# Gates of two token blocks by indirect transfers, those of the third by matmul

## The reference, cut to what matters

```python
def peer_ffn(xn, w_query, sub_keys, u, v):
    q = (xt @ w_query).reshape(T, H, 2, PEER_HALF)
    s = jnp.einsum('thpd,hpkd->thpk', q, sub_keys)
    top_s, top_i = lax.top_k(s, K)
    cand_s = (top_s[:, :, 0, :, None] + top_s[:, :, 1, None, :]).reshape(T, H, K * K)
    cand_i = (top_i[:, :, 0, :, None] * PEER_KEYS + top_i[:, :, 1, None, :]).reshape(T, H, K * K)
    best_s, best_pos = lax.top_k(cand_s, K)
    expert_idx = jnp.take_along_axis(cand_i, best_pos, axis=-1)
    gate = jax.nn.softmax(best_s, axis=-1)
    ...
        act = jnp.einsum('td,ted->te', x_blk, u[i_blk])
        hid = jax.nn.gelu(act, approximate=False) * g_blk
        return jnp.einsum('te,ted->td', hid.astype(v.dtype), v[i_blk])
```

## Time and profile before

| | |
|---|---|
| median of three runs | 2800.8 us |
| profiled execution, its own time | 2805.82 us |
| its span | 2804.1 us |
| PE / DVE / ACT / POOL busy | 2650.5 / 2014.8 / 1292.7 / 647.6 us |
| PE mean granted clock | 0.978 |
| query stage | 302 to 376 us |
| U stage | 376 to 1098 us |
| V stage | 1098 to 1597 us |

### The profile page before, as it was taken

One profiled execution on the slowest core, in us unless ns is written; L12 is line 12 of the kernel. 1 busy time (PEld: TensorE's weight loads), 2 busy tenths in 40 slices (PEclk: granted clock), 3 DMA queues, 4 the chain that ended last, 5 costly groups with the idle time before them and its releaser, 6 DMA issues. The chain is left out here.

```text
span 2804.1 us, 40190 instructions
## 1 busy us (share of the span) xinstructions
PE 2650.5 (95%) x14361; PEld 1355.1 (48%) x14563; DVE 2014.8 (72%) x3246; ACT 1292.7 (46%) x1379; POOL 647.6 (23%) x479
## 2 busy tenths in 40 slices
PE   6988999999999999999999899999999799999994
PEld 3464544444455554444444354455554455555552
DVE  4545778886688886888888864365643688888885
ACT  5432323323444443333333343345432488878884
POOL 0000000000010103888888400000000322332221
PEclk9988999999999999999999999999999799999997
DMA  5301334334365657999999723212213599999994
GB/s 195 106 31 46 113 113 158 144 147 150 135 221 184 223 181 253 348 364 363 368 363 370 288 106 105 91 61 76 76 46 150 192 388 400 402 397 397 393 397 149
DMA packets 129055, 609.08 MB, mean 217 GB/s; under 512 B 17328, under 2 KB 33712, under 8 KB 79296
## 3 DMA queue, kind: packets, MB, share of 16 engines
q1 hardware_dynamic: 57312, 411.62, 38.5%
q0 software_dynamic: 45024, 149.00, 15.1%
q10 hardware_dynamic: 26624, 47.19, 5.0%
HBM read 539.59 MB, written 68.16 MB: 217 GB/s over the span
## 5 line engine op out<-in xcount | busy, mean ns | idle before, releaser
L696 PE MATMUL ps<-a_lo,w_hi 128*128 128x512 bf16 (+3 forms) x1732 | 637.4, 370 | 4.9 <-issue 1.2
L697 PE MATMUL ps<-a_hi,w_lo 128*128 128x512 bf16 (+3 forms) x1737 | 639.1, 370 | 1.6 <-issue 0.2
L695 PE MATMUL ps<-w_hi,arena 128*128 128x512 bf16 (+1 forms) x1582 | 603.7, 382 | 23.1 <-ACT arena L1619 14.6
L695 PE MATMUL ps<-a_hi,w_hi 128*128 128x512 bf16 (+3 forms) x1685 | 619.2, 370 | 4.9 <-issue 2.1
L696 PE MATMUL ps<-w_lo,arena 128*128 128x512 bf16 (+1 forms) x1583 | 603.6, 381 | 3.1 <-DVE arena L2037 2.2
L697 PE MATMUL ps<-w_hi,arena 128*128 128x512 bf16 (+1 forms) x1583 | 603.5, 381 | 0.9
L1927 DVE TENSOR_TENSOR w_lo<-w_st,w_hi 128x2048 bf16<-128x2048 f32 x127 | 290.9, 2290 | 176.9 <-ACT w_hi L1405 140.6
L1405 ACT ACTIVATE w_hi<-w_st 128x2048 bf16<-128x2048 f32 x127 | 242.3, 1908 | 318.0 <-PE ps L697 304.8
L1411 ACT ACTIVATE xn<-ps 128x512 f32<-128x512 f32 x128 | 76.5, 597 | 428.4 <-PE ps L697 428.4
L697 PEld LDWEIGHTS ps<-a_hi,w_lo 128*128 128x128 bf16 x1760 | 172.6, 98 | 195.5 <-issue 2.7
L695 PEld LDWEIGHTS ps<-w_hi,arena 128*128 128x128 bf16 (+1 forms) x1600 | 166.6, 104 | 207.6 <-issue 20.7
(11 more groups left out here) (391 smaller groups left out, 3748.3 us busy)
## 6 DMA issues: line engine op xcount, KB each, us to landing
w_st<-in_w_all SPq DMA_DIRECT2D x260, 1024.0 KB
arena<-in_w_all SPq DMA_DIRECT2D x64, 1024.0 KB
act_dram<-xn POOLq DMA_DIRECT2D x64, 512.0 KB, 2.9
xn<-in_w_all SPq DMA_DIRECT2D x32, 1024.0 KB, 9.3
arena<-act_dram ACTq DMA_DIRECT2D x64, 384.0 KB
gate_dram<-arena POOLq DMA_DIRECT2D x7, 3072.0 KB, 19.3
arena<-gate_dram ACTq DMA_DIRECT2D x64, 336.0 KB
a_hi<-in_w_all SPq DMA_DIRECT2D x16, 1024.0 KB, 9.1
```

The lines of the kernel that those rows point to most:

```text
L695: pe.matmul(dst, l_hi, r_hi, start=start, stop=False)
L696: pe.matmul(dst, l_hi, r_lo, start=False, stop=False)
L697: return pe.matmul(dst, l_lo, r_hi, start=False, stop=stop)
```

## The change

- PE builds the gate matrix for block 3 only: 16 gate tiles in chunks 43 to 58, one a chunk, placed between the chunk's two tiles. The one-hots of a tile are made by DVE in the chunk before. Three transposes in chunk 41 replace nine.
- The units of scores are given a period of 14 chunks: 8 chunks with a unit, 6 without. The units of block 1 lie in chunks 2 to 9, of block 2 in 16 to 23, of block 3 in 30 to 37. The softmax is done block by block.
- For blocks 1 and 2 DVE adds, for each slot, the gates of all slots of the same token with the same expert (`share`: 128 instructions a block with `accum_out`, 32 a chunk, in chunks 12 to 15 and 26 to 29), and works out the place of each in the matrix (`places`). A slot whose expert came in an earlier head is sent to a spare cell.
- POOL writes them: 128 indirect transfers a block (`spread`), each of 128 cells of 4 B, six a chunk behind the store of activations, from chunk 16 on.
- So the matrix has to be zero before. ACT issues 14 stores of zeros, 1.57 MB each, seven in the query stage and one in each of the U chunks 0 to 6.
- `gate_dram` is now one row of 336 tokens per expert; the gates of block 3's first 80 tokens go there by two pairs of stores (in chunks 48 and 59), each store 8192 pieces of 160 B. The last 48 tokens stay in `g_st` as before.
- The loops over the U chunks are written out; `products` multiplies rows without groups. ACT waits for the last spread in chunk 62. A semaphore of the forget gate (`f_xs`) is merged with another.

```diff
+T_SPREAD = 2 * P
+GATE_TILES = [(0, t) for t in range(0, 40, 8)] + [(1, t) for t in range(80, P, 8)] + [(0, t) for t in range(40, 80, 8)]
+FIRST_TILE_AT = 43
+GATE_ROW = T_SPREAD + P - GT
+PERIOD = 14
+SPREAD_FROM, SPREAD_PER_CHUNK = 16, 6
...
+            def store_gates(tiles, first):
+                pool.wait_ge(g_out, 4 + 2 * tiles)
+                by_pair = g_st[:, 0, :, 0:40].rearrange("p (n j) t -> p j n t", j=2)
+                for j in range(2):
+                    at = j * GATE_ROW + T_SPREAD + first
+                    pool.dma_start(gate_rows[:, :, at:at + 40].rearrange("n p t -> p n t"), by_pair[:, j, :, :]).then_inc(g_stored, 16)
...
+            def spread(k):
+                b, j = divmod(k, SLOTS)
+                if j == 0:
+                    pool.wait_ge(place_done, b + 1)
+                pool.indirect_dma_start(gate_cells, bass.IndirectOffsetOnAxis(ap=place[:, b, j:j + 1], axis=0),
+                                        shared[:, b, j:j + 1], None).then_inc(g_spread, 16)
...
+            for n in range(N_U):
+                store_activations(n)
+                if n == FIRST_TILE_AT + 5:
+                    store_gates(5, 0)
+                if n == FIRST_TILE_AT + len(GATE_TILES):
+                    store_gates(len(GATE_TILES), 40)
+                if n >= SPREAD_FROM:
+                    for k in range(k, min(k + SPREAD_PER_CHUNK, 2 * SLOTS)):
+                        spread(k)
+                    k += 1
...
+            def zero_gates(part):
+                cells = gate_dram[0:GATES].rearrange("(p a x) -> p a x", p=P, x=TB * SLOTS)
+                act.dma_start(cells[:, part * ZEROS:(part + 1) * ZEROS, :],
+                              gate_t.unsqueeze(1).to_broadcast([P, ZEROS, TB * SLOTS])).then_inc(g_zero, 16)
...
+            for n in range(N_U):
+                unit = unit_of(n)
+                if unit is not None:
+                    scores(unit, unit % PH, slice(unit // PH * P, (unit // PH + 1) * P))
+                expert_tile(n, 0)
+                at = n - FIRST_TILE_AT
...
+                if 0 <= at < len(GATE_TILES):
+                    gate_tile(at)
+                expert_tile(n, 1)
...
+            def share(b, h):
+
+                if h:
+                    dve.drain()
+                    dve.memset(weight[:, (h - 1) * PTOP:h * PTOP], EARLIER)
+                    dve.drain()
+                for j in range(h * PTOP, (h + 1) * PTOP):
+                    if j % SAME == 0:
+                        dve.drain()
+                    dve.scalar_tensor_tensor(same[:, j % SAME, :], expert, expert[:, j:j + 1], weight, ALU.is_equal, ALU.mult,
+                                             accum_out=shared[:, b - 1, j:j + 1])
```

More of the change, by code:

```diff
@@ L574, in _ @@
[L574 to L586, removed]
@@ L962, in _ @@
                     for a, src in enumerate((key1, key2, score)):
[L963 to L964 removed]
+                        last = pe.transpose(ps[:, 4 + a, 0:P], src[:, (TB - 1) * P:TB * P], ident[:, :])
                     last.then_inc(slot_tp, 1)
[L966 to L983, removed]
@@ L1418, in _ @@
[L1418 to L1440, removed]
-                                       ps[:, 2 + 2 * (at % 2) + bank, :].rearrange("p (t k) -> p t k", t=4), ACT.Copy).then_inc(g_out, 1)
@@ L1442, in _, with gelu_tile @@
-            with act.Fori(4, 7) as i:
-                for c in range(8):
-                    experts_and_gates(i, c)
-            for c in range(8):
-                experts_and_gates(7, c)
-                if c == 6:
-                    act.wait_ge(g_stored[0], 16 * 5)
-                    act.wait_ge(g_stored[1], 16 * 4)
-                    for n in range(2):
-                        load_experts(act, 0, n)
+            def gelu_tile(n, t):
+                if t == 0 and n >= 2:
+                    act.wait_ge(u_stored[n % 2], 16 * (n // 2))
+                act.wait_ge(u_done, 2 * n + t + 3)
+                act.activation(u_st[:, n % 2, t, :], ps[:, t, :], ACT.Gelu).then_inc(u_out, 1)
@@ new lines, in gates_out @@
+            def gates_out(at):
+                b, first = GATE_TILES[at]
+                first -= 80 if b else first // 40 * 40
+                if at == 11:
+                    act.wait_ge(g_stored, 32)
+                for bank in range(2):
+                    act.wait_ge(g_done, 2 * at + bank + 5)
+                    tok = slice(first + bank * 4, first + bank * 4 + 4)
+                    act.activation(g_st[:, b, :, tok].rearrange("p k t -> p t k"),
+                                   ps[:, 2 + 2 * (at % 2) + bank, :].rearrange("p (t k) -> p t k", t=4), ACT.Copy).then_inc(g_out, 1)
@@ new lines, in _ @@
+            for n in range(N_U):
+                unit = unit_of(n)
+                if unit is not None:
+                    dve.wait_ge(s_done, unit + 1)
+                lo_in_loop(n, C_U + n + AHEAD)
+                if unit is not None:
+                    best_keys(unit % PH)
+                    if unit % PH == PH - 1:
+                        b = unit // PH
+                        block_slots(b)
+                        if b:
+                            soft_start(0 if b == 1 else b, b + 1)
+                if n in SOFT_END_AT:
+                    b = SOFT_END_AT[n]
+                    soft_end(0 if b == 1 else b, b + 1)
+                    if b < TB - 1:
+                        share_start(b)
+                    else:
+                        rows_of_block_0()
+                for b in range(1, TB - 1):
+                    part = n - last_unit_at(b) - 3
+                    if 0 <= part < 4:
+                        share(b, 2 * part)
+                        share(b, 2 * part + 1)
+                        if part == 3:
+                            places(b)
+                if n == TURN_AT + 1:
+                    slots()
+                if 0 <= n + 1 - FIRST_TILE_AT < len(GATE_TILES):
+                    gate_one_hots(n + 1 - FIRST_TILE_AT)
```

283 lines of the change are left out of this document (159 added, 124 removed).

## The result

The kernel after takes 2781.7 us (median of 4 runs, 2778.56 to 2785.62) against 2799.6 us for the kernel before beside it (4 runs, 2797.51 to 2802.88). The ratio is 0.9936, interval 0.9917 to 0.9955: 18 us faster. The profiled span falls from 2804.1 to 2782.8 us, by 21.3 us. The forecast was 2776 us and -25 us, so the direction and the range (2766 to 2812) held, and the gain is some 4 us (profiles) to 7 us (medians) smaller.

What follows compares the result with a forecast made beforehand. PE's own instruction list was taken to bound the U stage. Terms: -28.9 gate tiles, -0.7 transposes, +4 gate stores, about +0.6 queueing, -25 us in all: 2780.8 us profiled, 2776 us as median, range 2766 to 2812.

Steps and rivals of the forecast that it cites:

- What bounds the kernel: U stage: PE's own instruction list; what leaves it is worth its full time if nobody else becomes late.
- the sum of tiles and transposes: PE in the U stage: 32 gate tiles save 28.9 us and six transposes 0.7 us, -29.6 us together.
- Zeroing: Query stage and first U chunks: 14 zero stores, 22 MB, fit beside other loads; cost 0, bounds 0 to 3 us.
- Spreads: POOL, U stage: six indirect transfers a chunk, one caught by a long DVE instruction; cost 0, bounds 0 to +53 us.
- rival 1: U stage: spreads at 1.60 + 0.30 us make POOL the bound, net +23 us, 2824 us; chance 0.17.
- rivals 1 and 4: Rival 4, DMA queue in the U stage: the spreads' four-byte writes choke it, 70 us, 2841 us; chance 0.05.
- Shares: DVE: 128 comparisons a block over four chunks, 0.21 to 0.39 us each; cost taken 0, bounds 0 to 16 us.
- the 17 us stated as free: DVE may lag 17 us after its shares at no cost: scores are due two chunks later, weights three.
- The two gate stores: Chunks 48 and 59: back-to-back pairs, 15 us of engine time each, delay activation stores; cost 4 us, bounds 0 to 24.
- Rival 3: Gate store pairs cost per piece, 24 ns whatever its size: 24 us of stalls, 2795 us at most; chance 0.11.
- no PE wait of more than 1 us: Sign that the forecast is right: PE never waits longer than 1 us from chunk 2 to 58.
- Written-out loops: U chunk loops, with the merged semaphore: 0, bounded by the 4.9 us that PE's loads idle for issue before.

Runs made afterwards that it cites:

- apart: Kernel after with the two stores of each gate pair issued two chunks (first pair) and one chunk (second pair) apart; 2771.8 us, ratio to before 0.9894.
- thin pieces: Kernel after with all 8192 pieces per gate store cut from 160 B to 32 B, the other gates left out; 2769.4 us, ratio to before 0.9898.
- before_unrolled: Kernel before with only its loops over the U chunks written out; 2797.4 us against 2800.1 us, ratio 0.999.

## Why the prediction was right, and where it was off

**What bounds the kernel: right.** The U stage is PE's instruction list. `apart` shows the list with nobody late: 681.9 us against 710.9, -29.0; the sum of tiles and transposes said -29.6. Rows of 10.36 and 11.26 us stand in the trace as foretold.

**Zeroing, 0: right.** A zero store landed after 8.5 us (median of 14), the share rose to 0.67 between 387 and 484 us instead of "0.8", and PE lost nothing there. Twice the bytes cost some 4 us.

**Spreads, 0: right, and with it rivals 1 and 4 wrong.** The line group of the spreads in the kernel after, in the manner of the earlier trace rows (count | busy us, mean ns | idle before):

```profile
L627 POOL DMA_INDIRECT gate_dram<-arena x256 | 313.9, 1226 | 85.3 <-issue 79.3 <-DVE arena L2034 6.0
```

1.23 us on average, against 0.94 + 1.7 / 6 = 1.22 by the forecast's terms, rival 1's 1.60 and the 1.69 from which it would cost. The median is 0.958 us and the longest 2.96. Most chunks have one that meets the long DVE instruction, as assumed, and the time above the median makes 1.6 us a chunk, against 1.7. The contention rule of the Trainium skill (SBUF — State Buffer, Who interferes with whom) was weighed with a doubt about its second half, that each spread would hold up DVE as well, and the doubt holds: with spreads on POOL the 127 DVE splits (L1970) lie between 2271 and 2328 ns, so the transfer waits and the DVE instruction does not. A spread that starts under such a split ends 0.83 us after it (the one at 891.92, under the split from 891.74 to 894.03, as much as the one at 926.51), and one that is already running when the split begins takes its usual 0.96 us. Four-byte writes do not choke: from 546 to 663 us the DMA share is 0.45, spreads, activations and weights together.

**Shares, 0: right by its slack.** DVE's timeline, two comparisons in a row, and its splits at the start and at the end of block 2's four chunks of shares:

```profile
512.04 0.34 DVE L2007 SCALAR_TENSOR_TENSOR arena<-arena 128x128 f32<-128x128 f32 x1
512.31 0.08 DVE L2007 DVE_READ_ACCUMULATOR arena<-arena 128x1 f32 x1
512.31 0.35 DVE L2007 SCALAR_TENSOR_TENSOR arena<-arena 128x128 f32<-128x128 f32 x1
...
655.85 2.29 DVE L1970 TENSOR_TENSOR w_lo<-w_st,w_hi 128x2048 bf16<-128x2048 f32 x1 [7.09 <-ACT w_hi L1454]
...
710.27 2.28 DVE L1970 TENSOR_TENSOR w_lo<-w_st,w_hi 128x2048 bf16<-128x2048 f32 x1
```

An accumulator read (0.08 us) does follow each comparison, but the next comparison starts together with it, 0.27 us after the last: in the lower half of the 0.21 to 0.39 given. DVE needs 710.27 - 655.85 = 54.4 us for four chunks in which PE needs 4 x 10.36 = 41.4, so it falls 13 us behind. That is less than the 17 us stated as free, PE waits neither for a low part nor for scores, and leaving all of it out gives 0.6 us. Whether 17 is the right limit was not tried.

**The two gate stores, 4 us: the term that was mis-sized. It measured 14.6 us** (U stage of the kernel after less that of `apart`; the two losses of PE add up to 14.4). The forecast put both stores "back to back" into the queue and let the next activation store queue behind 15 us of engine work. The engine work was right (14 ns a piece measured, 15 used, and the alternative of "24 ns a piece whatever its size" falls). What failed is the words "issued back to back": in the kernel after and its repetition the second store of a pair starts 15.3 to 16.9 us after the first, with thin pieces 14.7 and 12.5, and in `apart`, where the second of the last pair is due one chunk later, it stands 7.3 us until 16.3 us are over. Everything behind it on POOL, six spreads and the store that ACT waits for, moves by as much. The kernel before could not show it: its gate stores lie four chunks apart (six tiles each, three tiles in two chunks). Rival 3 named the right places (PE gaps at chunks 51 to 52 and 62 to 63) with half of the cause: with the pairs on ACT's queue the pieces do the same work, and 3.8 us are lost with ACT's hold included; with thin pieces POOL stands, and nothing is lost. The landing of a second store, which it put at 35 us or more, is not in the trace. The sign "no PE wait of more than 1 us" failed at these chunks. Its rule from the Trainium skill (DMA: Bandwidth & Descriptors, Specifications), small pieces paying for a read-modify-write below 512 B, does not make them alike here: 7 ns at 32 B, 14 at 160 B and, from the earlier trace rows, 24 at 384 B.

The backlog of spreads is not the cause either: at the second pair the last spread was issued at 1025.40, before the first of its stores, and that pair still stands 12.52 us and opens a gap of PE no smaller than the first (5.57 us against 4.93).

**Written-out loops, 0: off by 2.2 us to the good side.** The 2.2 us lie inside the 4.9 us given as a bound. The cost lay in entering the loops, and behind the second Gelu `before_unrolled` is no faster than before (705.7 us to the last in both).

**The sum.** -29.0 for PE's list, +14.6 for the two pairs, -2.2 for the loops: -16.6. The span shows -21.3. The 4.7 left are 2.1 us before the U stage, where ACT's last query instruction starts at 374.10 instead of 376.18, and 2.6 us behind its last Gelu. Runs of the kernel before alone differ by 5 to 13 us, and the part behind the last Gelu differs by 5 us among kernels that are the same there; the cause of these 4.7 us stays open. That the total came so near is in part luck: the pairs were off by 10.6 us, and 2.2 + 4.7 us were given back by things that stood at nothing in the sum.

## What to carry to other kernels

A DMA that is free for the DMA engines can still stop the engine that issues it: with thousands of pieces per transfer, count pieces in that engine's queue, and keep two such transfers apart by more than the time that the first needs, above all when something that others wait for is issued behind them. When a stall moves to a place that looked safe, read the issuing engine's timeline for a long idle stretch that names no releaser, or for one long issue. Leave-out experiments (no stores, half of the pieces, same pieces with fewer bytes) separate room in a queue from work on the engines where the trace of one kernel cannot.

## What the runs showed of the hardware

- POOL's queue takes a store of 8192 pieces in 2.8 us of issue, then small ones at once; a second one of that size waits until 15 to 17 us after the first began (12.5 to 14.7 with pieces of 32 B). Two of 4096 pieces (1.7 us each) go without a wait. ACT's queue takes the first store of 8192 in 0.38 us, and the second, right behind it, holds ACT for 9.02 us.
- A piece costs about 7 ns of one DMA engine at 32 B, 14 at 160 B and 24 at 384 B.
- An indirect transfer of 128 cells of 4 B costs its issuer 0.94 us as a gather and 0.96 as a scatter, plus 0.30 us to the next. One that starts under a DVE subtraction of two SBUF tiles ends 0.83 us after it; the DVE instruction keeps its 2.29 us.
- A DVE instruction with an accumulated sum has a read of 0.08 us behind it, which the next one hides: 0.27 us from one to the next at 128x128.
- After gaps of 4.9 to 5.9 us PE comes back at the lower clock level for 2.9 to 5.7 us; the granted clock of the 18 us around a gap is 0.81 or 0.91.
- A wait of ACT of 8.89 us named "remote", after which it is 3.5 us late with no loss for PE, was seen in the kernel after near 965 us; it is not explained.
